# Experts by fetched token rows in a two-layer decoder step: picked rows by indirect DMA, scatter once a pair

## The chip, the cores and the metric

The kernel runs on one core of a Trainium2 chip. The metric is the time of one execution on the device in microseconds. A core has five engines with instruction rows of their own: TensorE (PE in the profile, its weight loads PEld), VectorE (DVE), ScalarE (ACT), GpSimd (POOL) and SyncE (SP), which here only issues the DMAs of the weights. They order each other by semaphores.

## The reference

One step of a two-layer decoder for 256 prompt tokens and 8 sample tokens (264 together), D_MODEL 1024, all in float32. Each layer has a mixing part, attention into 256 memory tokens, and a channel mixer: a dense one in layer 0, and in layer 1 the two best of eight experts.

```python
def swiglu(x, wg, wu, wd):
    return (jax.nn.silu(x @ wg) * (x @ wu)) @ wd

def moe(x, router_w, wg, wu, wd):
    logits = (xt @ router_w).astype(jnp.float32)
    top_v, top_i = lax.top_k(logits, TOP_K)
    gates = jax.nn.softmax(top_v, axis=-1)
    combine = jnp.sum(jax.nn.one_hot(top_i, N_EXPERTS, dtype=jnp.float32) * gates[..., None], axis=1)
    for e in range(N_EXPERTS):
        out = out + combine[:, e:e + 1].astype(x.dtype) * swiglu(xt, wg[e], wu[e], wd[e])
```

An expert has 1024 x 1408 weights for the gate, as many for the up product, and 1408 x 1024 for the down product. The input of the experts and of the router is the RMS-normalised x.

## The kernel before

Weights and activations that enter a large product are split in a high part, rounded to the type fp32r, and a low part, the rest; a product is then three (high by high, low by high, high by low; `product`, L597). ScalarE makes the high part of a weight unit (L1035 dense, L1288 experts), VectorE the low part (L1422, L1723), which frees its ring slot. High and low parts have three buffers each, so ScalarE may start on unit j + 3 when TensorE has used unit j. An expert is 24 units of 704 KB (16 of gate and up, 8 of down), in a ring of six slots that SyncE fills (L551 to L569).

Layer 1 ends with the attention's output projection `mo` (four pairs of outputs, `project_pair`), then, in a row: squares and their sum over features (L628), root (L1048), reciprocal (L1417), normalised x (L1730), router logits (L857, plain float32), the transposed tokens in high and low part (L865, L1277, L1763), the best two experts by VectorE (L1743 to L1756), the position of each token in its expert's list by small products (L875, L1766 to L1774), and the gather matrices (`gather_matrix`, L1777).

Experts go in pairs p with sides a and b; the first pair, a loop over the middle two and the last are written apart. For a pair, `gather` (L879) multiplies tokens (high and low) by two 0/1 matrices of 128 slots, 48 products of 256 columns, into four banks X0 to X3, whose high and low parts ScalarE and VectorE make (L1294, L1801). An expert (`expert`, L922 on TensorE, L1307 on ScalarE, L1811 on VectorE) then makes gate and up in four groups of 352 columns (banks G0, U0 to G3, U3; 24 products for each bank), ScalarE the silu (L1322), VectorE the product (L1827); its hidden rows are turned by 11 transposes in three steps T0, T1, T2 (L919, parts L1300 and L1808) and go through the down product (banks D0, D1). The previous expert's output is brought back to the tokens: VectorE makes a matrix of the gate weights (`scatter_matrix`), TensorE turns it by three transposes (bank S, L900), ScalarE copies it (L1305), and eight plain float32 products (16 records, L911; banks C0 to C7) are added to x by VectorE (`combine`, L1795).

All banks are eight PSUM banks in turn: a tile takes the bank of the tile eight places earlier, once that is read. What each engine does is a fixed row, written by hand: `upto(k)` on ScalarE and VectorE makes the parts up to unit k - 1 (units 24 to 26 are the next expert's first three). Behind the last expert come `combine`, the final norm and the output.

## Time and profile before

| | |
|---|---|
| median of 3 runs (lowest, highest) | 1186.4 us (1185.22, 1195.95) |
| the profiled execution | 1184.99 us |
| its span | 1183.2 us |
| mean granted clock of TensorE | 0.97 |
| TensorE, VectorE, ScalarE busy | 1107.1, 796.9, 642.5 us |
| read from HBM | 265.83 MB, 230 GB/s over the span |

The routing stage lies between 668.9 and 710.9 us, the experts between 710.9 and 1160.2 us. A record of a plain float32 product stands twice in the trace, one of an fp32r product or of a transpose once. Times of matmul records overlap: what a product costs is the distance from start to start, not its length.

### The profile page before, as it was taken

Reading aid. Unit: us, or ns where it says so; the run is one execution under the profiler, and the core shown is the slowest. Engines: PE = TensorE matmul, PEld = TensorE weight load, DVE = VectorE, ACT = ScalarE, POOL = GpSimd, SP = SyncE. Lnnn points to the kernel's source line nnn. Section 1 sums busy time; section 2 is a strip of 40 time slices with the busy share of each in tenths; the row PEclk is TensorE's granted clock in tenths of the full one; section 3 lists DMA queues with packets and bytes.
Section 4 is the critical chain, followed back from the end, with each engine's and each line's share of the span. In section 5 each row is a group of like instructions: output and inputs, shape, how many; then the busy total and the mean of one; then the engine's idle time right before and its main releaser. Section 6 shows DMA issues by size and latency. Waiting matters only on the chain.

```text
span 1183.2 us, 19963 instructions
## 1 busy us (share of the span) xinstructions
PE 1107.1 (94%) x7698; PEld 1027.8 (87%) x7698; DVE 796.9 (67%) x1137; ACT 642.5 (54%) x848; POOL 18.4 (2%) x38
## 2 busy tenths in 40 slices
PE   6998998899999999998987889999999999999995
PEld 5998985799999999998865879898989899889984
DVE  5698643566555665986532547886888788878884
ACT  5676443464434445575432426775766667566762
POOL 0010000000000000000000000000000000000000
PEclk8999999999999999999998958999999999999998
DMA  8444588656555555544687326995989598869861
GB/s 333 145 158 140 161 305 339 228 155 193 181 185 182 182 178 173 164 144 137 215 324 276 147 73 227 337 368 189 364 290 362 195 360 300 329 220 365 308 257 39
DMA packets 64276, 273.00 MB, mean 231 GB/s; under 512 B 7328, under 2 KB 7584, under 8 KB 63552
## 3 DMA queue, kind: packets, MB, share of 16 engines
q1 hardware_dynamic: 62352, 264.33, 63.5%
q0 software_dynamic: 1408, 7.12, 1.7%
q8 instruction: 58, 0.95, 0.3%
q10 hardware_dynamic: 432, 0.38, 0.1%
q14 instruction: 26, 0.21, 0.1%
HBM read 265.83 MB, written 5.98 MB: 230 GB/s over the span
## 4 chain that ended last, share of the span: by engine, by line
PE 69%; DVE 16%; ACT 6%; DMA 4%; issue 3%; SPq 1%; DVEq 0%; ACTq 0%
PE bank L603 10%; PE bank L605 10%; PE bank L604 10%; PE bank L600 9%; PE bank L601 9%; PE bank L602 9%; DVE wl L1422 4%; DMA ring<-dense 4%; ACT wh L1035 2%; PE bank L890 2%; PE bank L628 2%; DVE rstd L1417 1%; DVE wl L1723 1%; DVE sq L1433 1%; PE bank L891 1%
## 5 line engine op out<-in xcount | busy, mean ns | idle before, releaser
L1723 DVE TENSOR_TENSOR wl<-ring,wh 128x1408 fp32r<-128x1408 f32 x192 | 310.3, 1624 | 60.5 <-ACT wh L1288 60.4
L1422 DVE TENSOR_TENSOR wl<-ring,wh 128x1024 fp32r<-128x1024 f32 x170 | 206.8, 1223 | 178.4 <-ACT wh L1035 177.7
L1288 ACT ACTIVATE wh<-ring 128x1408 fp32r<-128x1408 f32 x189 | 261.4, 1383 | 85.8 <-PE bank L605 85.5
L600 PE MATMUL bank<-xh,wh 128*128 128x264 f32 x928 | 271.5, 293 | 23.6 <-DVE xl L1438 9.8
L1035 ACT ACTIVATE wh<-ring 128x1024 fp32r<-128x1024 f32 x170 | 179.1, 1058 | 163.9 <-PE bank L602 141.3
L601 PE MATMUL bank<-xl,wh 128*128 128x264 f32 x928 | 267.2, 288 | 0.0
L602 PE MATMUL bank<-xh,wl 128*128 128x264 f32 x928 | 266.6, 287 | 0.0
L604 PE MATMUL bank<-wh,xl 128*128 128x352 f32 (+4 forms) x736 | 244.0, 332 | 0.0
L600 PEld LDWEIGHTS bank<-xh,wh 128*128 128x128 f32 x928 | 178.4, 192 | 31.8 <-issue 18.4
L601 PEld LDWEIGHTS bank<-xl,wh 128*128 128x128 f32 x928 | 178.8, 193 | 0.1
L602 PEld LDWEIGHTS bank<-xh,wl 128*128 128x128 f32 x928 | 178.3, 192 | 0.0
L603 PE MATMUL bank<-wh,gathered_hi 128*128 128x352 f32 x512 | 167.4, 327 | 2.1 <-DVE xl L1801 1.7
L605 PE MATMUL bank<-wl,gathered_hi 128*128 128x352 f32 x512 | 165.3, 323 | 0.0
L604 PEld LDWEIGHTS bank<-wh,xl 128*128 128x128 f32 x736 | 139.5, 190 | 5.7
L603 PEld LDWEIGHTS bank<-wh,gathered_hi 128*128 128x128 f32 x512 | 96.8, 189 | 3.8 <-issue 2.2
L605 PEld LDWEIGHTS bank<-wl,gathered_hi 128*128 128x128 f32 x512 | 96.8, 189 | 0.0
L600 PE MATMUL bank<-hidden_hi,wh 128*128 128x264 f32 (+1 forms) x304 | 86.6, 285 | 3.3 <-DVE wl L1422 1.7
L601 PE MATMUL bank<-hidden_lo,wh 128*128 128x264 f32 (+1 forms) x304 | 85.9, 283 | 0.0
L602 PE MATMUL bank<-hidden_hi,wl 128*128 128x264 f32 (+1 forms) x304 | 85.7, 282 | 0.0
L603 PE MATMUL bank<-wh,xh 128*128 128x512 f32 (+3 forms) x224 | 79.9, 357 | 0.0
L605 PE MATMUL bank<-wl,xh 128*128 128x512 f32 (+3 forms) x224 | 79.1, 353 | 0.0
L600 PEld LDWEIGHTS bank<-hidden_hi,wh 128*128 128x128 f32 x304 | 57.2, 188 | 4.1 <-issue 4.0
(231 smaller groups left out, 1370.6 us busy)
## 6 DMA issues: line engine op xcount, KB each, us to landing
ring<-experts SPq DMA_DIRECT2D x192, 704.0 KB, 5.9
ring<-dense SPq DMA_DIRECT2D x234, 512.0 KB, 4.1
o_k<-kv POOLq DMA_DIRECT2D x2, 1024.0 KB, 4.5
o_v<-kv POOLq DMA_DIRECT2D x2, 1024.0 KB, 7.6
x<-xT SPq DMA_DIRECT2D x2, 528.0 KB, 5.0
o_y<-sq SPq DMA_DIRECT2D x4, 264.0 KB, 2.1
gatew<-gate_w POOLq DMA_DIRECT2D x2, 512.0 KB, 8.2
mem<-memT SPq DMA_DIRECT2D x1, 1024.0 KB, 13.3
```

Source lines behind the costliest of these rows:

```text
L600: mm(out, s_hi, m_hi, start=start, stop=False)
L601: mm(out, s_hi, m_lo, start=False, stop=False)
L602: return mm(out, s_lo, m_hi, start=False, stop=stop)
L603: mm(out, s_hi, m_hi, start=start, stop=False)
L604: mm(out, s_lo, m_hi, start=False, stop=False)
L605: return mm(out, s_hi, m_lo, start=False, stop=stop)
L628: i = mm(b[:, 0:T], ones[:, :], sq[:, m, :], start=(m == 0), stop=(m == KC - 1))
L890: mm(out, tokh[0:rows, t, f0:f0 + P], slots, start=(t == 0), stop=False)
L1035: A(wh[:, k % NBUF, 0:UNIT], raw(u), ACT.Copy).then_inc(hi_ready, 1)
L1288: A(wh[:, jj % NBUF, :], eraw(jj % ESLOTS), ACT.Copy).then_inc(ehi_ready, 1)
L1422: V.tensor_tensor(wl[:, k % NBUF, 0:UNIT], raw(u), wh[:, k % NBUF, 0:UNIT].bitcast(F32), ALU.subtract)\
L1723: V.tensor_tensor(wl[:, jj % NBUF, :], eraw(jj % ESLOTS), wh[:, jj % NBUF, :].bitcast(F32), ALU.subtract)\
```

## The change

What it does, part by part:

- The router reads x times the gains `norm_ffn` (ScalarE, `xg`), not the normalised x; its products stand between the last pairs of `mo`. The 1/rms of each token comes from small products of squares with a column of ones (`token_squares`) and scales the two best logits' difference, and later the silu, the up product and the output through per-slot scalars `now`.
- The tokens (with gains) are turned in two halves, copied once by ScalarE, and written by GpSimd's queue to a tensor `token_rows` in HBM.
- Slot matrices `sel` (0/1, float32) times token numbers give the list of token numbers of each expert; the first pair's list is made first (I0: six products with one column), those of all eight with weights and 1/rms after it (I1: 24 products with three columns). GpSimd's queue then fetches the 128 rows of each expert by indirect DMA (`picked`), a pair ahead.
- `gather` is 16 transposes of the picked rows. The transposed weight matrix (S) is gone.
- The expert's output is scaled and split in high and low part (`out_low`). The scatter is done once a pair, as 32 fp32r products with 0/1 matrices that VectorE makes in full width.
- The hidden rows are turned in four steps: T0 and T1 ahead of the last gate, T2 between the last gate and up, T3 behind the first unit of the down products.
- Experts with over 128 tokens go in two more passes, not one; on these inputs the kernel before does not run its second pass.

```diff
+            out += [("mo", l, m) for m in range(6)]
             out += [("lg", l, t) for t in range(3)]
-            out += [("tk", l, t, hp) for t in range(3) for hp in range(2)]
+            out += [("tk", l, t, 0) for t in range(3)]
+            out += [("mo", l, m) for m in range(6, KC)]
+            out += [("tk", l, t, 1) for t in range(3)]
+            out += [("sst", l)]
...
-    HIDDEN = ["G0", "U0", "G1", "U1", "G2", "U2", "T0", "S", "G3", "U3", "T1"]
+    SIDE = ["G0", "U0", "G1", "U1", "G2", "U2", "T0", "T1", "G3", "T2", "U3", "D0", "T3", "D1"]
+    TURNS = [(0, 2), (2, 5), (5, 8), (8, FEC)]
     COMBINE = [f"C{c}" for c in range(KC)]
     GATHER = [f"X{i}" for i in range(4)]
-    OUTPUT = ["T2", "D0", "D1"]
-    MID = ["a" + x for x in HIDDEN + COMBINE + OUTPUT] + ["b" + x for x in HIDDEN + COMBINE + GATHER + OUTPUT]
-    FIRST = ["a" + x for x in HIDDEN + OUTPUT if x != "S"] + [x for x in MID if x[0] == "b"]
+    NUMBERS = ["I0", "I1"]
+    AT = SIDE.index("D0")
+    MID = ["a" + x for x in SIDE[:AT] + COMBINE + SIDE[AT:]] + ["b" + x for x in SIDE[:AT] + GATHER + SIDE[AT:]]
...
+            for s in range(3):
+                project_pair("mo", l, s, xhi, xlo, T)
+            logits(0, 4)
+            turn_tokens(0, 0, 4)
+            project_pair("mo", l, 3, xhi, xlo, T)
+            logits(4, 6)
+            logits(6, KC)
+            turn_tokens(1, 4, KC)
+            def token_squares(ts):
+                n = tiles[("sst", l)]
+                b = take_bank(n) if 0 in ts else bank(n)
+                for t in ts:
+                    t0, rows_t = TOK[t]
+                    for c in range(KC):
+                        i = mm(b[0:rows_t, t:t + 1], sq[:, c, t0:t0 + rows_t], ones[:, 0:1], start=(c == 0), stop=(c == KC - 1))
+                if 2 in ts:
                     full(i, n)
+            pe.wait_ge(sq_ready, KC * (3 * l + 3))
+            token_squares([0])
...
+            token_squares([1, 2])
...
-                pe.wait_ge(gsel_ready, p + 1)
+                pe.wait_ge(picked_loaded, 32 * p + 32)
                 for x4 in range(4):
                     n, more = num(f"X{x4}")
                     b = take_bank(n, more)
                     for c in range(2):
-                        out = b[:, c * 2 * CAP:(c + 1) * 2 * CAP]
-                        for t, (t0, rows) in enumerate(TOK):
+                        for side in range(2):
                             f0 = (2 * x4 + c) * P
-                            slots = gsel[0:rows, t, :, :].rearrange("p b s -> p (b s)")
-                            mm(out, tokh[0:rows, t, f0:f0 + P], slots, start=(t == 0), stop=False)
-                            i = mm(out, tokl[0:rows, t, f0:f0 + P], slots, start=False, stop=(t == 2))
+                            i = nc.tensor.transpose(b[:, (2 * c + side) * CAP:(2 * c + side + 1) * CAP], picked[:, side, f0:f0 + P], ident)
                     full(i, n)
-            def turn_scatter(v, num):
-                n, more = num("S")
-                b = take_bank(n, more)
-                pe.wait_ge(wsel_ready, v + 1)
-                for t, (t0, rows) in enumerate(TOK):
-                    i = nc.tensor.transpose(b[:, t0:t0 + rows], wsel[0:rows, t, :], ident[0:rows, 0:rows])
-                full(i, n)
-            def scatter(num, before):
-                wait_read(pe, *num("S"))
+            def scatter(p, num, before):
+                pe.wait_ge(scat_ready, p + 1)
                 for u in range(2):
                     wait_read(pe, *before(f"D{u}"))
                 for c in range(KC):
                     n, more = num(f"C{c}")
                     b = take_bank(n, more)
-                    full(mm(b[:, 0:T], eo[:, c * P:(c + 1) * P], scat, start=True, stop=True), n)
-            def turn_hidden(num, i3):
-                n, more = num(f"T{i3}")
+                    for side in range(2):
+                        for part in range(2):
+                            i = mm(b[:, 0:T], eout[:, side, part, c * P:(c + 1) * P], scat[:, side, :], start=(side + part == 0),
+                                   stop=(side + part == 2))
+                    full(i, n)
...
+                        if g == 3 and gi:
+                            turn_hidden(num, 2)
...
                 turn_hidden(num, 0)
-                if not first:
-                    turn_scatter(v - 1, num)
+                turn_hidden(num, 1)
                 group(3)
-                turn_hidden(num, 1)
-                if not first:
-                    scatter(num, before)
+                if side == 0 and not first:
+                    scatter(p - 1, num, before)
                 if side == 1 and not last:
                     gather(p + 1, num)
-                turn_hidden(num, 2)
...
+                        if u + part == 0:
+                            turn_hidden(num, 3)
...
+                slot_numbers(ps, "I0", 0, 2, 0, 1)
+                if ps is main:
+                    pe.wait_ge(val_ready, 1)
+                slot_numbers(ps, "I1", 0, NE, 0, 3)
...
+                if side == 0:
+                    act.wait_ge(now_ready, p + 1)
...
-                    read(A(eo[:, u * 512:(u + 1) * 512], bank(n)[:, :], ACT.Copy), n)
+                    A(eout[:, side, 0, u * 512:(u + 1) * 512], bank(n)[:, :], ACT.Copy, scale=now[:, side, 1:2]).then_inc(eout_ready, 1)
...
+            elow(0, 0)
...
+            def slot_index(ps):
+                n, more = ps.prologue("I0")
+                wait_full(dve, n, more)
+                read(V.tensor_copy(slot[:, 0:2, 0], bank(n)[:, 0:6:3]), n)
+                wait_read(dve, n, more)
+                V.tensor_scalar(idx[:, 0:2], slot[:, 0:2, 0], -1.0, 0.0, ALU.add, ALU.max).then_inc(idx_ready, 1)
+            def slot_rest(ps):
+                n, more = ps.prologue("I1")
+                wait_full(dve, n, more)
+                dve.wait_ge(idx_ready, 2 * (2 * ps.p0 // NE) + 1)
+                read(V.tensor_copy(slot[:, :, :], bank(n)[:, 0:3 * NE].rearrange("p (v k) -> p v k", k=3)), n)
+                wait_read(dve, n, more)
+                V.tensor_scalar(idx[:, 2:NE], slot[:, 2:NE, 0], -1.0, 0.0, ALU.add, ALU.max).then_inc(idx_ready, 1)
+            def pair_scalars(p, p0):
+                V.tensor_copy(now[:, :, :], slot[:, bass.ds(2 * (p - p0), 2), :]).then_inc(now_ready, 1)
+                dve.wait_ge(now_ready, p + 1)
...
+                def out_low(u):
+                    n, more = num(f"D{u}")
+                    dve.wait_ge(eout_ready, 2 * v + u + 1)
+                    cols = slice(u * 512, (u + 1) * 512)
+                    read(V.scalar_tensor_tensor(out=eout[:, side, 1, cols], in0=bank(n)[:, :], scalar=now[:, side, 1:2],
+                                                in1=eout[:, side, 0, cols].bitcast(F32), op0=ALU.mult, op1=ALU.subtract), n)
...
                 turned_low(v, num, 0)
+                turned_low(v, num, 1)
+                upto(17)
+                turned_low(v, num, 2)
                 upto(18)
                 hidden(3)
-                turned_low(v, num, 1)
                 upto(19)
+                if side == 0:
+                    if not first:
+                        combine(num)
+                    scatter_matrix(p)
+                if side == 1 and not last:
+                    gathered_low(p + 1, num, 0, 2)
+                turned_low(v, num, 3)
+                upto(20)
+                if side == 1 and not last:
+                    gathered_low(p + 1, num, 2, 4)
+                upto(25)
+                out_low(0)
+                upto(26)
+                out_low(1)
+                upto(27)
...
+            slot_matrix(0, 2, 0)
+            elow(0, 1)
+            wait_read(dve, tiles[("sst", l)])
+            link(V.reciprocal(rs_tok, rms_tok))
+            link(V.tensor_tensor(ed, m8[:, :, 1], m8[:, :, 0], ALU.subtract))
+            V.tensor_tensor(ed, ed, rs_tok, ALU.mult).then_inc(lmax_ready, 1)
+            step(V.tensor_copy(val[:, :, :, 2], rs_tok.unsqueeze(2).broadcast_to([P, 3, NE * MAXB])))
+            slot_index(main)
...
+            signal(val_ready)
+            slot_matrix(2, NE, 0)
+            for j in range(2, NBUF):
+                elow(0, j)
+            slot_rest(main)
...
+            def pick(k, v):
+                for side in range(2):
+                    pool.indirect_dma_start(picked[:, side, :], None, rows, bass.IndirectOffsetOnAxis(idx[:, v + side:v + side + 1], 0))\
+                        .then_inc(picked_loaded, 16)
+            def run_pass(ps, k):
+                for i in range(ps.np):
+                    pool.wait_ge(idx_ready, 2 * k + (1 if i == 0 else 2))
+                    if i == 1:
+                        wait_full(pool, *ps.prologue("X3"))
+                    elif i > 1:
+                        n, _ = ps.first("bX3") if i == 2 else ps.middle(0)("bX3")
+                        wait_full(pool, n, 0 if i == 2 else i - 3)
+                    pick(k, 2 * i)
```

TensorE's row behind `mo`. Before: two rows of token transposes, the position products, the first products of the gather.

```order
L865 MATMUL bank<-con,sq 128x128 x16
L865 MATMUL bank<-con,sq 8x128 x8
L875 MATMUL bank<-kv,con 128x8
L875 MATMUL bank<-kv,ones 128x8
L875 MATMUL bank<-kv,con 128x8
L875 MATMUL bank<-kv,ones 128x8 x2
L875 MATMUL bank<-kv,con 128x8
L875 MATMUL bank<-kv,ones 128x8 x3
L890 MATMUL bank<-xh,hidden_hi 128x256
L891 MATMUL bank<-xh,hidden_lo 128x256
```

Now, from the first squares to the transposes of the picked rows (L919 squares, L932 positions, L944 the numbers I0 and I1, L957 the transposes):

```order
L919 MATMUL bank<-ones,sq 128x1 x8
L932 MATMUL bank<-route,con 128x8
L932 MATMUL bank<-route,ones 128x8
L932 MATMUL bank<-route,con 128x8
L932 MATMUL bank<-route,ones 128x8 x2
L932 MATMUL bank<-route,con 128x8
L932 MATMUL bank<-route,ones 128x8 x3
L919 MATMUL bank<-ones,sq 128x1 x8
L919 MATMUL bank<-ones,sq 8x1 x8
L944 MATMUL bank<-route,work 128x1 x6
L944 MATMUL bank<-route,work 128x3 x24
L957 MATMUL bank<-con,route 128x128 x16
```

The gather's products went, and 24 products of squares and 30 of numbers came in between; the logits and token transposes stand further up, around the last pair of `mo`.

VectorE's row at the end of the first pair, up to the loop over the middle pairs. Before (L1795 the additions, L1801 low parts of gathered rows, L1781 gather matrices):

```order
L1795 TENSOR_TENSOR x<-bank,x 128x264 x8
L1801 TENSOR_TENSOR xl<-bank,gathered_hi 128x512 x4
L1808 TENSOR_TENSOR xl<-bank,xh 128x384
L1787 TENSOR_SCALAR work<-con,kv 128x128 x3
L1723 TENSOR_TENSOR wl<-ring,wh 128x1408 x8
L1867 UNCONDITIONAL_BRANCH
L1867 ISA
L1781 ISA
L1781 TENSOR_SCALAR xh<-con,kv 128x128
```

Now (L1815 is the low part of a weight unit, L1933 `out_low`, L1881 the copy to `now`):

```order
L1815 TENSOR_TENSOR wl<-ring,wh 128x1408 x5
L1933 SCALAR_TENSOR_TENSOR expert_out<-bank,route,expert_out 128x512
L1815 TENSOR_TENSOR wl<-ring,wh 128x1408
L1933 SCALAR_TENSOR_TENSOR expert_out<-bank,route,expert_out 128x512
L1815 TENSOR_TENSOR wl<-ring,wh 128x1408
L1985 UNCONDITIONAL_BRANCH
L1985 ISA
L1881 ISA
L1881 COPY route<-route 128x6
```

The low part of the next expert's third unit now stands behind both output low parts, and the copy to `now` ahead of everything of the next pair; the additions are gone from this side.

## Rows read from the trace of the kernel before

**Rows 1.** The page, busy time, share of the span and instructions of each engine.

```profile
PE 1107.1 (94%) x7698; PEld 1027.8 (87%) x7698; DVE 796.9 (67%) x1137; ACT 642.5 (54%) x848; POOL 18.4 (2%) x38
```

**Rows 2.** Windows: length, busy time of each engine, granted clock, DMA share, GB/s.

```profile
940.00:1000.00 60.00, 59.20 (x349) 55.66 (x348) 51.76 (x52) 43.11 (x40) 0.00 (x0) 1.00 0.90 326
1015.00:1020.00 5.00, 5.00 (x34) 4.79 (x33) 4.75 (x5) 3.71 (x5) 0.00 (x0) 1.00 1.01 400
```

**Rows 3.** Timeline (start, length, engine, line), TensorE, a warm gather.

```profile
914.29 0.36 PE L890 MATMUL bank<-xh,hidden_hi 128*128 128x256 f32 x1 [0.71 <-DVE x L1795]
...
923.02 0.55 PE L919 MATMUL bank<-con,work 128*128 128x128 f32 x3
```

**Rows 4.** Timeline, TensorE, turns of hidden rows and weights, and a scatter.

```profile
785.73 0.60 PE L919 MATMUL bank<-con,work 128*128 128x128 f32 x4
786.16 0.54 PE L900 MATMUL bank<-con,work 128*128 128x128 f32 x3
786.62 0.43 PE L603 MATMUL bank<-wh,gathered_hi 128*128 128x352 f32 x1
...
857.11 3.73 PE L911 MATMUL bank<-kv 128*128 128x264 f32 x16
861.45 0.55 PE L919 MATMUL bank<-con,work 128*128 128x128 f32 x3 [0.61 <-DVE x L1795]
```

**Rows 5.** Timeline, all engines, from the last projection product to the first expert product.

```profile
668.81 0.28 PE L601 MATMUL bank<-xl,wh 128*128 128x264 f32 x1
668.93 0.28 PE L602 MATMUL bank<-xh,wl 128*128 128x264 f32 x1
...
675.80 8.75 PE L857 MATMUL bank<-rw,sq 128*128 128x8 f32 x48 [3.03 <-DVE sq L1730]
...
684.02 0.17 DVE L1739 COPY kv<-bank 128x8 f32<-128x8 f32 x1 [3.53 <-PE bank L857]
...
684.48 4.82 PE L865 MATMUL bank<-con,sq 128*128 128x128 f32 x24
...
686.57 0.18 DVE L1755 TENSOR_TENSOR kv<-kv 128x24 f32<-128x24 f32 x1
...
690.40 0.81 PE L875 MATMUL bank<-kv,ones 128*128 128x8 f32 x6
...
692.61 1.26 DVE L1781 TENSOR_SCALAR xh<-con,kv 128x128 fp32r<-128x128 f32 x6 [0.19 <-DVE kv L1773]
...
710.88 0.63 PE L603 MATMUL bank<-wh,gathered_hi 128*128 128x352 f32 x1 [1.72 <-DVE xl L1801]
```

**Rows 6.** Windows as in rows 2, in the routing stage.

```profile
676.00:680.00 4.00, 4.00 (x23) 3.81 (x24) 3.95 (x9) 1.09 (x1) 0.00 (x0) 0.50 0.02 4
688.00:692.00 4.00, 3.22 (x27) 2.79 (x25) 3.47 (x10) 3.15 (x5) 0.00 (x0) 0.93 0.01 2
```

**Rows 7.** Timeline, end of an expert's down products and start of the next pair.

```profile
824.63 1.39 ACT L1288 ACTIVATE wh<-ring 128x1408 fp32r<-128x1408 f32 x1 [0.58 <-PE bank L605]
...
825.92 0.58 ACT L1345 ACTIVATE kv<-bank 128x512 f32<-128x512 f32 x1
...
826.05 1.62 DVE L1723 TENSOR_TENSOR wl<-ring,wh 128x1408 fp32r<-128x1408 f32 x1 [0.34 <-ACT wh L1288]
...
826.47 1.38 ACT L1288 ACTIVATE wh<-ring 128x1408 fp32r<-128x1408 f32 x1
...
828.18 0.32 PE L603 MATMUL bank<-wh,gathered_hi 128*128 128x352 f32 x1
...
830.43 0.43 PE L603 MATMUL bank<-wh,gathered_hi 128*128 128x352 f32 x1 [0.18 <-DVE wl L1723]
```

**Rows 8.** Timeline, VectorE, one low part of gathered rows.

```profile
802.13 0.69 DVE L1801 TENSOR_TENSOR xl<-bank,gathered_hi 128x512 fp32r<-128x512 f32 x1 [0.67 <-ACT gathered_hi L1294]
```

**Rows 9.** DMA issues: count, KB each, median us to landing.

```profile
o_k<-kv POOLq DMA_DIRECT2D x2, 1024.0 KB, 4.5
gatew<-gate_w POOLq DMA_DIRECT2D x2, 512.0 KB, 8.2
```

More of the change, by code:

```diff
@@ L524, in trunk_kernel @@
         main = Pass(NT0, 0, NE)
-        extra = Pass(main.end, NE, NE * (MAXB - 1))
+        passes = [main]
+        for b in range(1, MAXB):
+            passes.append(Pass(passes[-1].end, NE * b, NE))
         @block.sync
@@ L1321, in silu @@
                         wait_read(act, *num(f"U{g - 2}"))
-                    read(A(esg[:, g % 2, :], bank(n)[:, 0:GW], ACT.Silu), n)
+                    read(A(esg[:, g % 2, :], bank(n)[:, 0:GW], ACT.Silu, scale=now[:, side, 2:3]), n)
+                if side == 0:
+                    act.wait_ge(now_ready, p + 1)
                 upto(4)
@@ L1824, in hidden @@
                     if g == 0 and not first:
[L1826 to L1832 removed]
+                        wait_full(dve, *before("T3"))
+                    read(V.scalar_tensor_tensor(out=eh[:, g * GW:(g + 1) * GW], in0=bank(n)[:, 0:GW], scalar=now[:, side, 2:3],
+                                                in1=esg[:, g % 2, :], op0=ALU.mult, op1=ALU.mult), n)
+                def out_low(u):
[4 more added lines that the diff above has]
+                                                in1=eout[:, side, 0, cols].bitcast(F32), op0=ALU.mult, op1=ALU.subtract), n)
                 upto(6)
@@ L1867, in run_pass @@
+                pair(p0, p0, ps.first, ps.prologue, first=True)
                 with dve.Fori(p0 + 1, p1) as p:
-                    pair(p, ps.middle(p), ps.earlier(p))
-                pair(p1, ps.last, ps.earlier(p1), last=True)
+                    pair(p, p0, ps.middle(p), ps.earlier(p))
+                pair(p1, p0, ps.last, ps.earlier(p1), last=True)
                 combine(ps.after)
-            gather_matrix(0)
-            for j in range(1, NBUF):
-                elow(0, j)
+            slot_matrix(0, 2, 0)
```

310 lines of the change are left out of this document (182 added, 128 removed).

## The prediction

> **What bounds the kernel now.** I read four views in this order: the page's busy shares, the windows and timeline of the expert stage, the timeline of the stage ahead of it (routing), and the DMA rows. The page puts TensorE at 94% of the span [rows 1]. In the expert stage it is the bound almost alone: in 940 to 1000 us it is busy for 59.20 of 60 us at full clock while VectorE has 51.76 [rows 2]. What is to be seen in the timeline there: products of 352 columns start every 0.16 us, the engine never waits for weights by more than 0.3 us, and the stretches that do no expert arithmetic are the gather (48 products, 914.29 to 923.02, 8.73 us a pair [rows 3]), the transposes of the weight matrix (0.46 us an expert) and the scatter (16 records, 857.11 to 861.45, 4.34 us an expert [rows 4]). Ahead of the stage stands a serial chain: the last attention projection starts its last product at 668.93, the first expert product comes at 710.88, 41.95 us later, and most of it runs at half clock [rows 5, 6].
>
> **The sum is made against the profiled execution**: 1184.99 us, of which 1183.2 are the span; the median of the runs is 1186.4, 1.4 us above it. That difference is smaller than any term below.
>
> **Part 1, gather, transposed weights and scatter on TensorE.**
> Gather: three of the four pairs have it inside the steady stretch. Removed: 3 x 8.73 = 26.2 us. Added: 16 transposes a pair. Four transposes take 0.43 us (785.73 to 786.16 [rows 4]), 0.11 us each, so 1.7 us a pair and 5.1 us in all. Gain 21.1 us.
> Transposed weights: three transposes from 786.16 to 786.62 [rows 4], 0.46 us, of which the change to products behind them stays; seven of them, 3.2 us.
> Scatter: seven in the steady stretch, 4.34 us each (with the wait of 0.61 us for VectorE's additions, which frees the bank), 30.4 us. In their place three scatters of 32 products with 264 columns; such products start 0.12 us apart (668.81 and 668.93 [rows 5]), so 3.9 us each, 11.6 us. Gain 18.8 us. VectorE's eight additions now run beside a scatter as long as they are, and only one in two experts has them.
> The turns of the hidden rows stay at 11 transposes an expert. The third goes between the last gate and up products, the fourth behind the first unit of the down products; each pays a change of kind, an estimate of 0.03 us, and none waits: the hidden rows of the last group are turned 3.8 us of down products before their chunks are used. Cost 0.5 us in all. At the tail the last scatter now waits for ScalarE's copy and VectorE's low part (0.58 and 0.69 us, [rows 7, 8]) where it waited for a copy of the transposed weights: 0.6 us later.
> Together 21.1 + 3.2 + 18.8 - 0.5 - 0.6 = 42.0 us.
>
> **Part 2, new waits on VectorE's row.** The chain that feeds TensorE is short: ScalarE makes the high part of a unit when the unit three earlier is used (1.38 us), VectorE the low part (1.62 us). Behind the last down product of an expert it reads in [rows 7]: high part of unit 26 from 824.63, copy of the output from 825.92, low part from 826.05 to 827.67; TensorE wants that unit at 828.18. So 0.5 us are to spare. Now VectorE's low part of the output (`out_low(1)`) stands ahead of that low part and needs ScalarE's copy, which ends at 826.5; it takes 0.69 us (a 128x512 subtraction, [rows 8]), and the unit is ready at 828.8 in place of 827.67: TensorE waits 0.65 us, at seven ends of experts, 4.6 us. At a pair's start ScalarE now waits for `now`, which VectorE copies after that low part: the next high part starts at 829.05 in place of 826.47, its low part ends near 832.1, and TensorE wants it at 830.8: 1.4 us, against the 0.2 us seen at 830.43 [rows 7], where the gather matrices stood. Three starts, 3.6 us. In an expert with a gather, two of the low parts of the gathered rows push the low part of unit 20 by 0.35 us beyond its use, three times, 1.0 us. Together 9.2 us. Each may be nought where VectorE runs ahead, or double where ScalarE too is late; ends 0 and 18.
>
> **Part 3, the opening.** Start of the last projection product was 668.93. Now 12 router products (24 records) and 12 transposes stand ahead of the last projection pair. Records with 8 columns cost 0.11 us at high clock (six in 0.81 us with the last one's tail) and 0.18 at half (48 in 8.75), transposes 0.1 to 0.2 (24 in 4.82) [rows 5]: 4.2 us, projection end 673.1. Then 1.2 us for the addition and the copy with gains and 0.7 for the last router products: logits at 675.0, where they were read at 684.02. The mask took VectorE until 686.75, 2.73 us: 677.8. TensorE has 12 transposes and 8 products of squares first, so the position products start near 679 and end at 681; VectorE has a low part of weights in that place (until 681.3), needs 1.4 us for slots and 1.26 for six compare matrices (the row at 692.61): 684. TensorE does 16 more products of squares and 6 with one column, 44 records, 5 to 8 us from 681, against VectorE's low part and ScalarE's roots: indices at 688.
> Rows: two row fetches on GpSimd's queue. No indirect transfer is in the trace; the nearest rows are GpSimd's 1 MB write, 4.5 us to landing, and its 0.5 MB load under load, 8.2 us [rows 9]. With 1.1 us for two issues, rows are there at 693.6 to 697.3.
> Beside that, TensorE needs the 24 products with three columns. They wait for the exponential (its step in the chain and six small ones behind it, some 3 us, 691) and for 18 compare matrices (3.8 us), and are 48 records of 0.11 to 0.18 us: done at 696.5 to 699.8. This, not the transfer, is late last. Then 16 transposes at half clock (3.2 us) and one copy and subtraction (1.4 us): first expert product at 702.5, 8.4 us earlier than 710.88. Ends: 698 with full clock throughout, 709 if the fetch or clock is at its worst, so 2 to 13 us. I take 8.4, nearest to the half-clock rows. The stretch at half clock at the head of the first expert I leave as long as it is.
>
> A rule that speaks against this part: TensorE is at 1.2 GHz for nearly all of 676 to 716 although it is busy there; in 688 to 692 it is granted 0.93 [rows 6]. The Trainium skill (TensorE: Matmul & The Clock Gate, Part 4) says that transposes do not raise the clock, and the change puts 40 transposes and many one-column products here. By it the opening would run at half clock to the end, the 709 end of my range; the rows say only that small products run at either level.
>
> **DMA.** A pair moves 48 units of 0.721 MB and now 1.05 MB of rows, 35.7 MB. A pair lasted 115 us and will last about 105, so 339 GB/s, and windows of 5 us carry up to 400 [rows 2]. I cost it at nothing: the ring of six units is the cover. If it sustained only the 326 GB/s of 940 to 1000 (where it also paused), a pair would take 109.5, 4.5 us more, 17 us in all.
>
> **Sum.** 1184.99 - 42.0 + 9.2 - 8.4 = 1143.8; on this execution's scale. The runs' median stands 1.4 us above it, less than any term is sure to; I give 1144.
>
> **Rivals.**
> Weights become the bound (a transfer in place of TensorE). For it: the DMA engines are 0.90 busy in 940 to 1000. Against: they pause while a gather runs, and no high part waited for a unit. 1144 + 17 = 1161. Chance 0.15.
> The opening gains nothing, since the fetch, the clock or the chain of roots and exponentials eats it: 1152. Chance 0.17.
> The new waits stay below 3 us since TensorE's own wait lets VectorE catch up, and the opening gains 12: 1134. Chance 0.18.
> Slower than before: GpSimd makes the row descriptors in software while VectorE is busy for some 90% of the time; if the pair's two fetches take longer than a pair, about 105 us, TensorE waits for each of three pairs, and the first is wholly exposed. It decides from the point where the exposed sum passes 42 us: at 55 us a fetch wholly exposed in the first pair, or 120 us a pair (15 x 3). At 60 us in the first pair the time is 1144 + 55 = 1199. Against it: plain transfers of that queue land in 4.5 to 8.2 us [rows 9]. Chance 0.04. The Trainium skill (SBUF — State Buffer, on the door of VectorE and GpSimd) says that a VectorE instruction in a two-port mode keeps GpSimd from writing descriptors until its end; VectorE's longest here is 1.62 us, so by it the fetch would be some us later, not 55. No row here shows it.
>
> **How the numbers follow.** The forecast, 1144, has 0.46; its own range is 1137 to 1150. What a measurement of this kernel can tell from no change is about 1%, 12 us. The range must leave 2 in 10 out: from 1130 (the favourable rival's lower side) to 1160 (the ring's side). Faster by over 1% needs less than 1174.5: all but the slower case and the far tail of the ring's, 0.94; within 1% 0.03; slower 0.03.
>
> **What would show it.** Right: three gaps of some 2 us between the copies of `now` and TensorE's fourth unit, 0.6 us ends of experts, scatters of 3.9 us in three places and one at the end, transposes of 1.7 us, first expert product near 702, DMA rate near 340 GB/s. Wrong: ScalarE's high parts waiting for ring transfers; TensorE waiting for picked rows; the clock at 0.5 long after the first expert product; low parts of the gathered rows last.

## The result, and the profile after

The changed kernel takes 1147.67 us (median of 4 runs, 1147.28 to 1149.94), beside 1190.22 us for the kernel before on the same chip: ratio 0.9645, 95% interval [0.9604, 0.9687]. The profiled execution took 1147.54 us, 1145.7 of them the span. The forecast was 1144.0, range 1130 to 1160, faster.

The page's first part, busy time of each engine (answers to [rows 1]):

```profile
PE 1069.2 (93%) x7638; PEld 1004.7 (88%) x7638; DVE 784.5 (68%) x1118; ACT 643.1 (56%) x858; POOL 29.4 (3%) x49
```

TensorE lost 37.9 us of work, about what the span lost (37.5): what was taken off the bound came off the time. (The row counts time at half clock too, so this agreement alone proves little; the doubled scatter below does.) The steady stretch, in windows as in [rows 2]:

```profile
800.00:900.00 100.00, 97.53 (x598) 92.71 (x598) 86.79 (x79) 72.93 (x70) 2.65 (x2) 1.00 0.92 339
900.00:1000.00 100.00, 97.20 (x592) 91.98 (x591) 87.09 (x78) 71.91 (x67) 0.00 (x0) 1.00 0.92 341
1000.00:1100.00 100.00, 97.32 (x588) 91.69 (x587) 87.19 (x79) 72.33 (x68) 0.00 (x0) 1.00 0.90 327
```

TensorE is idle for 2.5 to 2.8 of 100 us where it was idle for 0.80 of 60, the transfers run at 327 to 341 GB/s (339 was forecast), and the clock is full. What fills the idle time is read in TensorE's waits over 640 to 1146 us (total, times, longest):

```profile
PE bank L633 <- DVE wl L1815: 9.6, 14, 1.1
```

These 14 waits are for low parts of expert weights; none in this stretch is for a transfer. The timeline (start, length, engine, line) of the change from one pair to the next, against [rows 7]:

```profile
809.11 0.67 ACT L1423 ACTIVATE expert_out<-bank,route 128x512 fp32r<-128x512 f32 x1
809.81 0.75 DVE L1933 SCALAR_TENSOR_TENSOR expert_out<-bank,route,expert_out 128x512 fp32r<-128x512 f32 x1 [0.73 <-ACT expert_out L1423]
810.47 1.61 DVE L1815 TENSOR_TENSOR wl<-ring,wh 128x1408 fp32r<-128x1408 f32 x1
811.24 0.32 PE L635 MATMUL bank<-wl,gathered_hi 128*128 128x352 f32 x1
812.00 0.17 DVE L1881 COPY route<-route 128x6 f32 x1
...
812.24 0.40 PE L633 MATMUL bank<-wh,gathered_hi 128*128 128x352 f32 x1 [0.67 <-DVE wl L1815]
...
812.40 1.38 ACT L1369 ACTIVATE wh<-ring 128x1408 fp32r<-128x1408 f32 x1 [2.62 <-DVE route L1881]
...
815.49 0.43 PE L633 MATMUL bank<-wh,gathered_hi 128*128 128x352 f32 x1 [1.09 <-DVE wl L1815]
```

Read downwards: ScalarE copies the output (809.11), VectorE waits 0.73 us for it and makes its low part (809.81) before the low part of unit 26 (810.47), and TensorE stands 0.67 us at 812.24. `now`, the per-slot scalars of the pair, is copied behind that (812.00), so ScalarE, which waits for it, has stood 2.62 us when it starts its next high part, and TensorE stands again, 1.09 us at 815.49. Scatter and row transposes, which replace those of [rows 3, 4]:

```profile
841.43 4.05 PE L970 MATMUL bank<-xh,expert_out 128*128 128x264 f32 x32
...
845.38 0.50 PE L633 MATMUL bank<-wh,xh 128*128 128x512 f32 x1
```

The next kind of product starts 3.95 us after the scatter's start. The 16 transposes of a later pair take 1.75 us in the chain of waits:

```profile
789.18 1.75 PE bank L957 x16
```

The opening, timeline of all engines (against [rows 5]):

```profile
673.33 2.66 PE L889 MATMUL bank<-rw,work 128*128 128x8 f32 x24
675.67 0.51 DVE L1823 COPY route<-bank 128x8 f32<-128x8 f32 x3 [1.71 <-PE bank L889]
...
687.12 0.17 DVE L1868 TENSOR_SCALAR slot_index<-route 128x2 uint32<-128x2 f32 x1
...
688.12 1.03 POOL L2090 DMA_INDIRECT route<-token_rows,slot_index  x1 [8.80 <-DVE slot_index L1868]
688.64 11.75 PE L944 MATMUL bank<-route,work 128*128 128x3 f32 x48 [1.75 <-DVEq L1479]
...
700.32 3.68 PE L957 MATMUL bank<-con,route 128*128 128x128 f32 x16
...
705.72 0.63 PE L633 MATMUL bank<-wh,gathered_hi 128*128 128x352 f32 x1 [1.72 <-DVE xl L1900]
```

The clock granted in it (against [rows 6]):

```profile
676.00:680.00 4.00, 4.00 (x38) 3.91 (x38) 2.37 (x17) 3.39 (x5) 1.57 (x3) 1.00 0.33 133
680.00:684.00 4.00, 4.00 (x44) 3.96 (x43) 3.58 (x15) 3.23 (x3) 0.00 (x0) 0.77 0.87 316
...
688.00:692.00 4.00, 3.36 (x14) 3.29 (x15) 3.81 (x21) 0.00 (x0) 2.07 (x2) 0.50 0.64 210
```

The first expert product is 5.2 us earlier than the 710.88 of before; 0.5 of that was there at the first product of `mo`, ahead of everything that was changed (643.65 against 644.18). From that product to the first expert product it is 62.1 us for 66.7, so the opening gained 4.6. In it, 11.75 us go into 24 products with three columns each, 48 records.

### The profile page after: what moved, and what is told of

Read it like the earlier page. It is cut to its first block, busy times and chain, and to the rows that moved or that the text cites. A ratio compares the mean times of both kernels' runs of the same rounds, so it can differ in the third digit from the quotient of the medians.

```text
span 1145.7 us, 19837 instructions
## 1 busy us (share of the span) xinstructions
PE 1069.2 (93%) x7638; PEld 1004.7 (88%) x7638; DVE 784.5 (68%) x1118; ACT 643.1 (56%) x858; POOL 29.4 (3%) x49
## 4 chain that ended last, share of the span: by engine, by line
PE 66%; DVE 17%; ACT 7%; DMA 5%; issue 4%; SPq 1%; DVEq 0%; ACTq 0%
PE bank L633 10%; PE bank L630 9%; PE bank L635 9%; PE bank L634 9%; PE bank L631 9%; PE bank L632 9%; DVE wl L1501 5%; DMA ring<-dense 4%; ACT wh L1103 3%; DVE wl L1815 2%; PE bank L658 2%; DVE rstd L1496 1%; PE bank L970 1%; DVE sq L1512 1%; PE bank L944 1%
## 5 line engine op out<-in xcount | busy, mean ns | idle before, releaser
L1815 DVE TENSOR_TENSOR wl<-ring,wh 128x1408 fp32r<-128x1408 f32 x192 | 308.6, 1622 | 51.9 <-ACT wh L1369 49.8
L1501 DVE TENSOR_TENSOR wl<-ring,wh 128x1024 fp32r<-128x1024 f32 x170 | 206.7, 1224 | 178.1 <-ACT wh L1103 177.3
```

Source lines behind the costliest of these rows:

```text
L1501: V.tensor_tensor(wl[:, k % NBUF, 0:UNIT], raw(u), wh[:, k % NBUF, 0:UNIT].bitcast(F32), ALU.subtract)\
L1815: V.tensor_tensor(wl[:, jj % NBUF, :], eraw(jj % ESLOTS), wh[:, jj % NBUF, :].bitcast(F32), ALU.subtract)\
```

## The experiments

My theory: the span is TensorE's row, so each wait or product in it counts whole; the new waits are the two orders on VectorE and ScalarE that the prediction names; and in the opening the 48 thin records, not the fetch, are late last. The rivals: transfers or VectorE stand close behind and take over, or the fetch and the clock set the opening. All medians are of 4 to 7 runs. The changed kernel, run again for reference, gave 1149.49 where its first runs gave 1147.67, and the kernel before gave medians of 1187.58 to 1192.46 on the four chips of these experiments. So medians of different chips compare to some 2 to 5 us, and the waits and stretches in the profiles are the finer measure. The two waits and the doubled scatter ran on a chip on which the changed kernel itself did not.

> The changed kernel itself, unchanged, beside the other kernels of this call, so that small differences are read on one chip. Every theory: 1147.7 us within 0.3 per cent, and a profile with the same stalls on the low parts as in its first profile.

Measured: 1149.49 us (1146.67 to 1152.23), and the same 9.6 us in 14 waits.

### The two waits, one by one and together

The output's low part behind the low part of unit 26:

```
-                out_low(1)
                 upto(27)
+                out_low(1)
```

> VectorE splits the gate and up products of the second expert up to unit 26 before it copies the low part of the output, as the kernel before did; all else is the changed kernel. Theory (each new stall is a wait of TensorE for one VectorE copy that now stands behind another): the stalls of about 0.70 us at unit 26 that fall inside a pair go (four of the seven; at a pair's start the copy only moves in front of another wait), 4 x 0.7 = 2.8 us less than the changed kernel, so about 1144.9 us, and the rows of TensorE's waits on the low parts lose these four. Rival (the span is set by the weights' transfers or by VectorE's sum of work): under 1 us, since the stall would come back at the next wait.

ScalarE's wait for `now` behind the high part of the pair's fourth unit (the first three are made before the pair starts):

```
+                upto(4)
                 if side == 0:
                     act.wait_ge(now_ready, p + 1)
-                upto(4)
```

> ScalarE waits for the rows in token order behind its first four copies of the down products, not ahead of them. Theory: the three stalls of 1.0 to 1.1 us at the pairs' starts go and nothing takes their place: about 3.0 us less than the changed kernel, 1144.7 us. Rival (the wait is only moved, since the slot transposes or VectorE are late right behind it): under 1 us.

> Both of the two edits before. Theory: the seven stalls of 0.70 us and the three of 1.05 us go, with about 0.4 us left at each of three pair starts: 7 x 0.7 + 3 x 1.05 - 3 x 0.4 = 6.9 us less, 1140.8 us; that is more than the two edits one by one (2.8 + 3.0), since at a pair's start each stall hides the other. Rival (VectorE or the weights close behind): 2 us or less.

Measured: 1145.82 (1143.81 to 1152.36), 1146.39 (1141.78 to 1146.72) and 1140.61 us (1138.23 to 1145.36). TensorE's waits for these low parts in the expert stage, in this order:

```profile
PE bank L633 <- DVE wl L1815: 6.6, 7, 1.8
```

```profile
PE bank L633 <- DVE wl L1815: 7.0, 11, 1.2
```

```profile
PE bank L633 <- DVE wl L1815: 2.5, 6, 1.2
```

That is 3.0, 2.6 and 7.1 us less than 9.6, where 2.8, 3.0 and 6.9 were expected, and both together give more than the sum of the two, as foreseen. The longest wait of the first of the three kernels, 1.8 us, is the pair start, where one stall now stands for two. The longest of the other two, 1.2 us, is in the first expert, where the changed kernel had 0.65. The medians of the first two lie 1.3 to 3.7 us below the two medians of the changed kernel, within what chips differ by; what shows these two edits is the waits.

The time of the third fell by 7.1 us against the first runs of the changed kernel and 8.9 against the second. In the profiles, the stretch from the first expert product to the last down product went from 415.0 to 404.9 us (404.7 when run again), 10.2 less, where the waits account for 7.1. Two things make up about the rest. A stall costs more than its row says: products start 0.16 us apart, but the 812.24 one came 1.00 us after the one before it (811.24), so 0.84 us was lost where 0.67 is shown; for ten stalls that is an estimate of 1.6 us more. And TensorE was granted its full clock from the first expert product on, where the changed kernel ran its first 3.8 us of them at 0.50, an estimate of 1.9 us, which the edits were not made for. First the window of the changed kernel (first expert product at 705.72), then that of the third (at 708.36):

```profile
708.00:712.00 4.00, 4.00 (x23) 4.00 (x22) 0.82 (x1) 2.28 (x2) 0.00 (x0) 0.82 0.38 136
708.00:712.00 4.00, 3.64 (x23) 3.67 (x24) 0.33 (x1) 1.38 (x1) 1.27 (x2) 1.00 0.67 208
```

The first kernel shows the opposite: behind two of its three stalls at pair starts (1.76 us at 819.63, 1.75 at 925.42) the clock fell to 0.50 for some 3 us, which it did not behind the shorter stalls of the changed kernel. The window behind the one at 819.63:

```profile
820.00:824.00 4.00, 4.00 (x17) 4.00 (x16) 3.40 (x3) 2.06 (x2) 0.00 (x0) 0.57 0.82 252
```

The rival (a new bound close behind) falls: 2 us or less was its figure. Run once more, the kernel held its time:

> The kernel with both waits moved, once more, so that the next two kernels are read beside it on one chip. Every theory: 1140.6 us within 0.3 per cent.

Measured: 1139.98 us (1137.81 to 1142.83), beside 1187.58 for the kernel before.

### Is TensorE the bound: work added to it, bytes added to the queue

```
+                    for again in range(2):
                         for side in range(2):
                             for part in range(2):
```

> The scatter's 32 products are issued twice into the same banks in each of the four pairs; the output stays the same. Theory (TensorE's work is the bound in the middle of the kernel, so a scatter is worth its whole 3.9 to 4.1 us): 4 x 3.9 = 15.6 us more than the changed kernel, 1163.3 us. Rival (the weights' transfers or VectorE would have bounded soon): at most half of it, under 8 us more, because the added work would fill waits.

Measured: 1164.09 us (1161.28 to 1167.28), 16.4 above the first and 14.6 above the second runs of the changed kernel, both on other chips. The doubled scatter in the timeline, and the waits, which did not shrink to make room:

```profile
841.12 7.95 PE L971 MATMUL bank<-xh,expert_out 128*128 128x264 f32 x64
```

```profile
PE bank L633 <- DVE wl L1816: 9.6, 14, 1.1
```

3.90 us more for one scatter, four times, is 15.6 us, which lies between the two differences. The scatter's price in the sum is shown.

```
                         .then_inc(picked_loaded, 16)
+                    pool.indirect_dma_start(tokens[:, side, :], None, rows, ...)\
+                        .then_inc(picked_loaded, 16)
```

> Each fetch of 128 token rows is made a second time into a tile that nobody reads, and TensorE waits for both: 1.05 MB more in each pair. Theory (the transfers of the weights have slack, and GpSimd has a pair's time for the fetch): at most 1 us more, except for the first pair, where the doubled fetch may show by 1 to 3 us if it lands near 700. Rival (the weights' transfers are about to bound): 2.8 us more in each pair, 8 to 11 us in all, and waits of TensorE or ScalarE on transfers.

Measured: 1150.4 us (1148.55 to 1153.32), 0.9 above the changed kernel on the same chip, which is within the spread of either. Two steady windows, then ScalarE's only wait for a transfer in the experts and TensorE's wait behind it:

```profile
800.00:900.00 100.00, 96.28 (x588) 91.24 (x588) 86.35 (x77) 72.02 (x69) 0.73 (x1) 1.00 0.93 346
900.00:1000.00 100.00, 97.22 (x588) 91.75 (x587) 86.35 (x80) 71.73 (x67) 4.09 (x4) 1.00 0.94 348
```

```profile
ACT wh L1369 <- DMA ring<-experts: 1.5, 1, 1.5
```

```profile
814.64 0.40 PE L633 MATMUL bank<-wh,gathered_hi 128*128 128x352 f32 x1 [1.63 <-DVE wl L1815]
```

The engines moved 346 to 348 GB/s where they had moved 339 to 341. TensorE waited for no transfer directly, but once through ScalarE: a unit came late to the ring, the high part was made 1.53 us late, and TensorE stood 1.63 us where the changed kernel stood 0.67. All its waits for low parts are 10.5 us instead of 9.6. From the first expert product to the last down product it took 414.2 us, the changed kernel 415.0 and 414.6. The opening took 3.2 us more than in the changed kernel on the same chip (65.6 for 62.5), with no wait for the rows, and the stages ahead of it as much less. So at this rate the transfers are not the bound, but they are close enough to be seen once.

### The opening: the thin records, the fetch, or the clock

The records of experts 2 to 7 moved behind the first group of the first expert:

```
-                slot_numbers(ps, "I1", 0, NE, 0, 3)
+                slot_numbers(ps, "I1", 0, 2, 0, 3)
...
                 group(0)
+                if first:
+                    slot_numbers(first, "I2", 2, NE, 0, 3)
```

> The slot numbers of the first pair alone stand ahead of its rows (12 of the 48 records); those of the six later experts come after the first group of the first expert, in a bank of their own. Theory (the 48 thin records at half clock, 11.75 us, are what is late last in the opening; the rows land by 694 to 697): TensorE then has 2.9 us of them ahead, waits for the rows until they land, and the other 36 records cost about 4 us at the full clock later: first expert product 702 to 704 instead of 705.7, and 0 to 3 us less in all, about 1146.9 us. Rival (the landing of the rows was about as late as the records): first expert product as before, 705 to 706, and the 36 records on top, 2 to 4 us more than the changed kernel.

Measured: 1151.15 us (1148.54 to 1151.92), 1.7 above the changed kernel on the same chip. Timeline of the opening, and after it the window rows and the chain of waits where the 36 records stand:

```profile
688.92 2.99 PE L944 MATMUL bank<-route,work 128*128 128x3 f32 x12 [1.75 <-DVEq L1481]
...
695.08 3.68 PE L957 MATMUL bank<-con,route 128*128 128x128 f32 x16 [3.17 <-DMA route<-token_rows,slot_index]
700.50 0.63 PE L633 MATMUL bank<-wh,gathered_hi 128*128 128x352 f32 x1 [1.75 <-DVE xl L1909]
```

```profile
708.00:712.00 4.00, 4.00 (x29) 3.97 (x27) 2.78 (x2) 3.33 (x3) 0.00 (x0) 1.00 0.63 192
712.00:716.00 4.00, 4.00 (x22) 3.88 (x23) 2.40 (x3) 0.62 (x1) 0.00 (x0) 0.67 0.87 290
716.00:720.00 4.00, 4.00 (x15) 3.95 (x16) 0.35 (x2) 0.00 (x0) 1.14 (x2) 0.50 0.72 238
```

```profile
711.14 6.73 PE bank L944 x36
```

The first half holds: with 12 records ahead the rows are waited for (3.17 us), they land at 695.08, inside the 693.6 to 697.3 of the prediction, and the first expert product comes at 700.50 where the logits' products had started 0.4 us later than in the changed kernel. So the 48 records were late last, by about 5 us over the fetch. The second half falls: the 36 records took 6.73 us instead of 4, since the clock, 1.00 in the window from 708, was 0.67 and then 0.50 again while they ran, and the wide products after them ran at half clock too. A start 5.2 us earlier became 4.6 us later at the first scatter (846.0 against 841.4), 4.2 counted from the router's first product (663.9 against 663.6). The time is near the 2 to 4 us more of this run's rival, but not for its reason, a late landing.

Next, dummy products of 512 columns among the thin ones, to hold the clock (shown are those among the three-column products; 4, 2 and 6 more stand ahead of them):

```
...
                 for v in range(v0, v1):
+                    if ps is main and name == "I1":
+                        wide(1)
```

> In the opening, products of 512 columns whose result nobody reads stand among the thin ones (4 behind the squares, 2 and 6 at the two waits, one ahead of each six records of the slot numbers). Theory (thin products alone let the granted clock fall to 0.5 from 684 to 708, and wide ones between them keep it at 1.0): the rows of the slot numbers fall from 0.245 to about 0.12 us a record, the transposes and the first products behind them run at the full clock, and the kernel gains 3 us (0 to 6), 1144.7 us. Rival (the clock falls all the same, or the wide products only add): 3 to 5 us more.

Measured: 1151.32 us (1149.62 to 1153.44), 1.8 above on the same chip, not clear of the spread. In the profiles the stretch from the first product of `mo` to the first expert product grew from 62.5 to 66.5 us. Its windows and timeline:

```profile
688.00:692.00 4.00, 4.00 (x16) 3.40 (x15) 0.97 (x5) 1.83 (x5) 0.00 (x0) 0.61 0.54 184
692.00:696.00 4.00, 3.83 (x21) 3.06 (x22) 3.24 (x19) 0.00 (x0) 2.06 (x2) 1.00 0.16 24
...
700.00:704.00 4.00, 4.00 (x17) 3.72 (x16) 0.00 (x0) 0.00 (x0) 0.00 (x0) 0.50 0.56 180
```

```profile
694.15 0.50 PE L941 MATMUL bank<-xh 128*128 128x512 f32 x1 [0.17 <-DVEq L1492]
694.49 0.81 PE L956 MATMUL bank<-route,work 128*128 128x3 f32 x6
695.23 0.51 PE L941 MATMUL bank<-xh 128*128 128x512 f32 x1
...
700.73 0.80 PE L941 MATMUL bank<-xh 128*128 128x512 f32 x1
...
702.62 0.80 PE L941 MATMUL bank<-xh 128*128 128x512 f32 x1
```

A run of wide products brought the clock back to 1.00, and six thin records then fit between wide products 1.08 us apart; one wide product to six thin records did not hold it, and from 700 on the same group takes 1.89 us. Between the two theories: the clock is reached by wide work, but this dose cost more than it gave.

Last, the records in four portions: 12 ahead of the fetched rows, 12 in the wait for them, 12 in each expert of the first pair.

```
-                slot_numbers(ps, "I1", 0, NE, 0, 3)
+                slot_numbers(ps, "I1", 0, 2, 0, 3)
+                slot_numbers(ps, "J1", 2, 4, 0, 3)
...
                 group(1)
+                if spread:
+                    slot_numbers(spread, "ab"[side] + "I2", 4 + 2 * side, 6 + 2 * side, 0, 3)
```

> The changed kernel with the slot numbers of the later experts taken apart: those of the first two experts (12 records) ahead of the first rows, those of experts 2 and 3 (12) in the wait for these rows, those of 4 and 5 and of 6 and 7 (12 each) after the second group of the first and of the second expert. Theory (the 36 records in one piece made the granted clock fall again in the run that split them, which gave back its gain; twelve at a time do not, and cost 0.11 us each at the full clock): first expert product 5.8 us earlier than in the changed kernel, reckoned from the second half of the router's products, then 24 x 0.11 = 2.6 us for the records, 3.2 us less in all, 1146.3 us on the chip of the repeated run. Rival (the fall of the clock comes anyway, or any record behind a wide product costs what it did at the half clock): 0 to 3 us more than the changed kernel.

> Both waits moved, the slot numbers spread as in the kernel beside it, and the second half of the gathered low parts one unit later on VectorE. Theory: the gains add, since they lie in different stretches: 3.2 us from the opening and 3 x 0.3 = 0.9 us from the last stalls at unit 20, so 4.1 us less than the kernel with both waits moved, 1136.5 us. Rival (the opening gives nothing, as in the run that split the records): 0.9 us less or no gain.

> Both waits moved and the second half of the gathered low parts one unit later on VectorE; the slot numbers stand together in the opening, as in the changed kernel. Theory (spreading the slot numbers only traded 3.1 us in the opening for 3.0 us of records later, as the profile of the spread kernel has it): the three stalls of 0.29 us go, 0.9 us less than the kernel with both waits moved, and the rest of the 4.0 us by which the kernel with all three edits stood below it comes from the opening's clock and not from this edit: about 1139.1 us. Rival (the later low parts are worth more, for example by letting the next stretch start sooner): 3 to 4 us less, 1136 us.

Measured: spread alone 1147.2 us (1144.29 to 1150.49), with a ratio to the kernel before of 0.9636 where the changed kernel had 0.9645 and 0.964, so no gain is shown (3.2 us were expected); both waits moved, records spread and the low parts later 1135.95 us (1133.87 to 1138.08), 4.0 below the kernel with both waits moved on the same chip; the same without the spreading 1141.1 us (1140.55 to 1143.07) on another chip, where its theory had 1139.1 and its rival 1136. Timeline and chain of the spread kernel:

```profile
690.09 5.91 PE L946 MATMUL bank<-route,work 128*128 128x3 f32 x24 [1.75 <-DVEq L1484]
...
697.80 3.67 PE L959 MATMUL bank<-con,route 128*128 128x128 f32 x16 [1.80 <-DMA route<-token_rows,slot_index]
...
703.19 0.63 PE L635 MATMUL bank<-wh,gathered_hi 128*128 128x352 f32 x1 [1.72 <-DVE xl L1913]
```

```profile
721.53 1.50 PE bank L946 x12
```

Twelve records at a time left the clock at 1.00 from 712 to 728 and cost 0.125 us each, so that part of the theory holds. The rows landed at 697.8, later than the 695.1 of the split kernel (the first fetch was issued 1.2 us later there), and in the profile the gain of the opening, 3.1 us, is what the 24 later records take, 3.0: from the router's first product to the first scatter it is 178.1 us (664.2 to 842.3) against 177.9 in the changed kernel. The later low parts took the last stalls at unit 20 away (2.5 us in 6 waits became 1.6 in 3), yet the kernel that has them without the spreading was no faster than 1139.98 and 1140.61. So the 4.0 us by which the version with all three edits won on its chip are explained only to 0.9. Its profile bears out no more: from the first product of `mo` to the end it took 1094.2 us, the kernel with both waits moved 1092.1 and 1095.1 in its two profiles. The opening gained 4.1 us against the profile of the same chip (58.6 for 62.8) and the experts lost 5.3 (410.0 for 404.7), and the two executions are equal in length only because the untouched stages ahead of `mo` were 2.4 us shorter (1137.55 and 1137.81 us). These two executions were the second longest of the one kernel and the shortest of the other, so they do not settle it: how much of the 4.0 is chance stays open. It has the lowest median of all kernels here, but its ratio to the kernel before, 0.9546 [0.9502, 0.9589], is not told apart from those of the kernel with only both waits moved, 0.9552 [0.9508, 0.9596] and 0.9587 [0.9543, 0.9630].

## Why the prediction was right

The two profiled executions, stretch by stretch (us), beside what the sum has for each:

| stretch | before | now | difference | forecast |
|---|---|---|---|---|
| start to the first product of `mo` | 644.2 | 643.7 | -0.5 | 0 |
| to the first expert product | 66.7 | 62.1 | -4.6 | -8.4 |
| to the last down product | 448.5 | 415.0 | -33.4 | -33.4 |
| to the end | 23.9 | 25.0 | +1.1 | +0.6 |

Together -37.5 where -41.2 was forecast. So the mechanism held in the experts, where nine tenths of the gain lie, and the miss is in the opening.

**Part 1** held. Scatters of 3.9 us were priced and took 3.95; transposes of 1.7 took 1.75; the third and fourth turn cost no wait. That the stretch of the experts agrees to 0.1 us is in part luck: it holds a stall of 0.65 us that was not foreseen, and its first products ran at half clock for 3.8 us where they had 5.0 before, which gives back an estimated 0.6.

**Part 2** held in place and size. The waits of 0.65 us at the ends of experts were about 0.70 (0.67 at 812.24), the 1.4 us at pair starts were 1.1 (1.09 at 815.49), and the 0.35 us at unit 20 were 0.29; taking the orders back took them away. Two things were missed, both small: one more stall of 0.65 us inside the first expert (at 716.02, a place for which the sum has no term), and 1.77 us ahead of the last scatter, where copy and low part were priced at 1.27 (0.58 and 0.69):

```profile
1123.36 4.12 PE L970 MATMUL bank<-xh,expert_out 128*128 128x264 f32 x32 [1.77 <-DVE expert_out L1933]
```

**Part 3** is the mis-sized term: 8.4 us forecast, 5.2 measured from the start of the span, 4.6 from the first product of `mo`. The steps up to the indices came within 0.9 us (logits 675.67 for 675.0, indices at 687.3 for 688), the exponential's chain let the last records start at 688.64, earlier than the 691 forecast, and then the step "48 records of 0.11 to 0.18 us" failed: they took 11.75 us, 0.245 each, and ended at 700.4, where the forecast's own 702.5, less 3.2 for the transposes and 1.4 for the copies, puts them at 697.9. Against the 6.9 us left for them from 691 on they took 4.9 more, and the early start hid 2.4 of it, by luck. The 0.18 came from 48 records in 8.75 us at half clock [rows 5], which is a mean over two shapes. The row of that line, all its forms named, shows it:

```profile
L857 PE MATMUL bank<-rw,sq x48: 169/361/382, 675.8 to 684.4; 128*128 128x8 f32 x32, 128*8 128x8 f32 x16
```

A third of those records has a stationary tile of eight columns; the slot matrices always fill 128 (the forms are 128*128 and 8*128):

```profile
L944 PEld LDWEIGHTS bank<-route,work x60: 279/333/339, 683.9 to 700.0; 128*128 128x128 f32 x40, 8*128 8x128 f32 x20
```

32 records at 0.245 and 16 at 0.06 (an estimate: what is left of the 8.75, by 16) make the 8.75. The starts of the single records bear it out: on average 0.24 us to the next one behind a record with 128 stationary columns, 0.07 behind one with eight. So what a thin record costs goes by the columns of its stationary tile, whether that has 8 rows or 128. The transposes and the two copies behind the records took 0.7 us more than forecast; with 2.5 from the records that is the 3.2 us. The rule weighed there, from the Trainium skill (TensorE: Matmul & The Clock Gate, Part 4: transposes do not raise the clock), is not contradicted by the trace: the 12 transposes at 675.9 ran at 1.00 right behind wide products, the clock fell behind them and the thin records (0.77 in 680 to 684), and it stayed at 0.50 through the 16 transposes at 700 and rose only among the expert products (0.82 in 708 to 712). The opening did run at half clock to its end, as that paragraph of the prediction feared; it ended at 705.7 all the same, not at 709.

**The rivals.** Weights as the bound (1161): TensorE and ScalarE waited for no transfer in the experts, and with 1.05 MB more a pair ScalarE waited once. The slow descriptors (1199): GpSimd's issue of a fetch is 0.94 to 1.71 us in its rows, and the eight landed after 4.1 to 9.4 us. The opening that gains nothing (1152) and the favourable one (1134) were both off on the same term, from either side.

## What to carry to other kernels

Where one engine is the bound, a change to the order on another engine is worth what its last arrival does to that engine's row: find the instruction that now stands between a high part and a low part, and count it once for each place; two such stalls in a row hide one another, so they must be taken out together. Before a mean duration of a group is used as a price, look at its forms: what a thin product costs goes by the number of columns of its stationary tile, not by the one to eight that it streams. Thin products in one piece, put among wide ones, can bring the clock down again and lose what their absence gained elsewhere; twelve records at a time did not. And when two profiles are compared, compare them from the last product that the change cannot have touched: here the stages ahead of it differed by up to some 5 us from one execution to the next.

## What the hardware showed that was not expected

- A product with three or one moving columns and a 128-column stationary tile takes 0.245 us a record at the granted clock 0.50 (48 in 11.75) and 0.125 at 1.00 (12 in 1.50), also when the tile has only 8 rows.
- The clock fell from 1.00 to 0.50 in the middle of dense expert products, behind 36 such records (1.00 in 708 to 712 us, 0.67 in 712 to 716, 0.50 in 716 to 720). Six wide dummies from 687.7 and six more from 692.3 had it back at 1.00 in 692 to 696.
- It also fell among dense expert products behind an idle gap of TensorE of 1.76 us (0.57 in 820 to 824) and one of 1.75, and not behind a third of 1.49, nor behind gaps of 0.67 and 1.09 us that lay 3.3 us apart.
- A fetch of 128 rows of 4 KB by an indirect transfer is issued in some 1 us. The two of the first pair landed after a median of 5.5 us; the four issued while the rings moved 340 GB/s and VectorE was busy for 87% of the time landed after a median of 8.6.
